# Weight tiles that are split two split tiles ahead, in a two-block transformer kernel

## What is computed

```python
mod = einsum('bd,de->be', silu(c), w_ada) + b_ada         # 48 modulation tiles, "ada"
h = modulate(rms_norm(x, norm1_w), shift1, scale1)
q, k, v, r, a_lr, su, sv, g_a, g_b = split(h @ w_in)
o_gla = rms_norm(gla_chunked(q, k, v, log_a)) * silu(r)
o_sgu = spatial_gating(gelu(su), gelu(sv), ...)
x = x + gate1 * ((sigmoid(g_a) * o_gla + sigmoid(g_b) * o_sgu) @ w_out)
x = x + gate2 * peer(modulate(rms_norm(x, norm2_w), shift2, scale2), ...)
# second block, for each of two layers l
mod   = silu(c_2) @ w_ada_2[l] + b_ada_2[l]               # 48 tiles per layer, "ada2"
mod_c = silu(c_ctx_2) @ w_ada_2[l] + b_ada_2[l]           # from the same tiles
...
x = x + gt_f * rms((silu(hf @ w_gate) * (hf @ w_up)) @ w_down, g_ffn_post)
```

## Time and profile before

| | us |
|---|---|
| median of 3 runs | 2558.24 (2558.07 to 2560.07) |
| the profiled execution | 2554.62 |
| its span, first to last instruction | 2552.9 |
| PE busy | 2240.4 |
| DVE busy | 1735.4 |
| ACT busy | 1151.7 |
| mean granted TensorE clock | 0.93 of full |

### The profile page before, as it was taken

One profiled execution on the slowest core, in us unless ns is written; L12 is line 12 of the kernel. 1 busy time (PEld: TensorE's weight loads), 2 busy tenths in 40 slices (PEclk: granted clock), 3 DMA queues, 4 the chain that ended last, 5 costly groups with the idle time before them and its releaser, 6 DMA issues.

```text
span 2552.9 us, 37972 instructions
## 1 busy us (share of the span) xinstructions
PE 2240.4 (88%) x14746; PEld 2009.0 (79%) x14746; DVE 1735.4 (68%) x3402; ACT 1151.7 (45%) x1907; POOL 53.4 (2%) x65
## 2 busy tenths in 40 slices
PE   3897789999999999988878789699979978797997
PEld 3887689999988888887757566599879967566996
DVE  5665558889988887767675565577666665664554
ACT  2532244555555554534344345444444444354443
POOL 1000000000000000000000000000000000000000
PEclk9998889999999999989977869799999999898999
DMA  7636545664468887767532100377657743102653
GB/s 278 196 127 205 177 147 180 220 218 135 145 197 283 268 278 235 245 188 227 181 126 77 35 33 17 124 229 235 213 183 246 256 160 115 58 1 89 186 187 117
DMA packets 137971, 435.04 MB, mean 170 GB/s; under 512 B 15360, under 2 KB 38144, under 8 KB 137280
## 3 DMA queue, kind: packets, MB, share of 16 engines
q1 hardware_dynamic: 109424, 396.93, 48.1%
q10 hardware_dynamic: 25776, 23.97, 2.8%
q0 software_dynamic: 2592, 11.70, 1.2%
HBM read 418.91 MB, written 13.63 MB: 169 GB/s over the span
## 4 chain that ended last, share of the span: by engine, by line
PE 65%; DVE 14%; issue 10%; ACT 7%; DMA 3%; POOL 1%; ACTq 0%; POOLq 0%; DVEq 0%; SPq 0%
PE bk L1650 63%; DVE SPL L1082 4%; PE bk L1656 3%; ACT SPL L737 2%; DVE R L1082 2%; ACT R L739 1%; DVE R L1091 1%; ACT R L737 1%; DVE ST L1097 1%; DVE RAW L1116 1%; POOL ST L639 1%; DMA RAW<-in_ada 1%; DVE R L1088 1%; DVE R L1086 1%; DMA RAW<-in_peer 1%
## 5 line engine op out<-in xcount | busy, mean ns | idle before, releaser
L1082 DVE TENSOR_TENSOR SPL<-RAW,SPL 128x1024 fp32r<-128x1024 f32 (+1 forms) x614 | 742.7, 1219 | 388.2 <-ACT SPL L737 387.2
L737 ACT ACTIVATE SPL<-RAW 128x1024 fp32r<-128x1024 f32 (+1 forms) x614 | 638.8, 1051 | 387.9 <-PE bk L1650 294.5
L1650 PE MATMUL bk<-HH,SPL 128*128 128x256 f32 x3840 | 753.3, 290 | 47.0 <-DVE SPL L1082 38.5
L1650 PEld LDWEIGHTS bk<-HH,SPL 128*128 128x128 f32 x3840 | 623.9, 195 | 61.0 <-issue 30.0
L1650 PE MATMUL bk<-SPL,WHL 128*128 128x512 f32 x2328 | 553.2, 392 | 13.2 <-DVE SPL L1082 9.5
L1650 PE MATMUL bk<-HL,SPL 128*128 128x256 f32 x1920 | 548.7, 286 | 0.0
L1650 PEld LDWEIGHTS bk<-SPL,WHL 128*128 128x128 f32 x2328 | 431.2, 189 | 103.7 <-issue 13.1
L1650 PE MATMUL bk<-SPL,HH 128*128 128x256 f32 (+1 forms) x1664 | 335.0, 303 | 62.9 <-DVE SPL L1082 48.3
L1650 PEld LDWEIGHTS bk<-HL,SPL 128*128 128x128 f32 x1920 | 374.3, 195 | 1.9 <-issue 0.2
L1650 PEld LDWEIGHTS bk<-SPL,HH 128*128 128x128 f32 x1664 | 285.2, 211 | 72.9 <-issue 55.9
L737 ACT ACTIVATE R<-bk 128x512 f32<-128x512 f32 (+5 forms) x376 | 186.6, 508 | 341.1 <-PE bk L1650 309.9
(11 more groups left out here) (126 smaller groups left out, 1993.6 us busy)
## 6 DMA issues: line engine op xcount, KB each, us to landing
RAW<-in_peer SPq DMA_DIRECT2D x256, 512.0 KB, 4.8
RAW<-in_ada SPq DMA_DIRECT2D x144, 512.0 KB, 4.7
RAW<-in_ffn SPq DMA_DIRECT2D x132, 512.0 KB, 4.0
RAW<-in_win SPq DMA_DIRECT2D x96, 512.0 KB, 4.4
RAW<-in_ffd SPq DMA_DIRECT2D x66, 512.0 KB, 4.2
RAW<-in_wout SPq DMA_DIRECT2D x32, 512.0 KB, 4.0
kept<-TMP ACTq DMA_DIRECT2D x88, 128.0 KB, 3.4
TMP<-kept ACTq DMA_DIRECT2D x66, 128.0 KB, 5.3
```

The source lines that it names most:

```text
L737: ins = e.activation(out, in_, func, bias=bias, scale=scale)
L1082: e.tensor_tensor(out, a, b, op).then_inc(*dve.up(*points))
L1650: ins = e.matmul(out, lhsT, rhs, start=start, stop=stop, skip_group_check=True)
```

## The change

The lead is counted in split tiles. `PASSED[n]` is the number of split tiles up to place n, and the new function `lead(n)` gives the place behind the second split tile after n, but not more than NRAW places on. Modulation tiles in between are prepared along the way and don't count. Ahead of the first split tile the old rule stays. Both loops, on ACT and on DVE, use it; the branch for the early PEER steps gets a `max`.

```diff
+import itertools
...
 SPLIT_NO = {n: k for k, n in enumerate(SPLITS)}
+PASSED = list(itertools.accumulate(IS_SPLIT))
+
+
+def lead(n):
+
+    return min(SPLITS[min(PASSED[n] - 1 + LEAD, len(SPLITS) - 1)], n + NRAW) + 1 if PASSED[n] else n + LEAD + 1
...
-                ahead = max([ahead] + [n + LEAD + 1 for n in CHUNKS[step]])
+                ahead = max([ahead] + [lead(n) for n in CHUNKS[step]])
...
                 if step[0] != "pe":
-                    ahead = max([ahead] + [n + LEAD + 1 for n in CHUNKS[step]])
+                    ahead = max([ahead] + [lead(n) for n in CHUNKS[step]])
                 elif step[2] == 2:
-                    ahead = CHUNKS[("pe", step[1], 0)][0] + LEAD + 1
+                    ahead = max(ahead, lead(CHUNKS[("pe", step[1], 0)][0]))
```

## The result

The changed kernel takes **2497.61 us** (median of 4 runs, 2494.03 to 2500.03) against 2558.15 us (4 runs, 2556.24 to 2560.07) on the same chip: a ratio of 0.9762, 95% interval 0.9745 to 0.9779. That is 60.5 us less. The profiled executions differ by 57.6 us (2554.62 and 2496.97). The forecast was 2505 with a range of 2486 to 2528, so direction and time came out as forecast. It will turn out that three of its terms did not.

The account below looks back on a forecast made before the run. The prediction took PE's waits for split weight tiles, in the gates caused by order, as the bound. Gains of 33 + 2.4 + 6 + 6 + 6 = 53 us from the median 2558.2 gave 2505 us, range 2486 to 2528.

Parts of the forecast that it names:

- What bounds the kernel, and the gates: Gates r1 to gb3: order bounds, not an engine; 11 periods shrink from 10.4 to 7.4 us, gaining 33 us.
- the ring: RAW slots in the gates: landing, copy, subtraction, then next load; claimed as next bound, 7.4 us per turn.
- Behind the last gate: Two wout subtractions ahead of A2 and the merges now run under gb3's matmuls: 2.4 us, 0 if late.
- v and sv: First projections: of 8.4 us of waits, only steps next to a modulation tile are cured: 6 us, 2 to 8.
- Peer alone: PEER from 735 to 975 us: PE is full already, so 32 moved tiles buy nothing.
- (d): Peer onward: moved subtractions delay hidden activations on DVE; half of 183 tiles costing PE loses 104 us: 2620; chance 0.04.
- Woven part: PEER woven with context projections, 60 moved tiles: 2 us at the longest wait plus 4 elsewhere: 6 us, -3 to 12.
- Output projection and FFN: Layer 0, 91 moved tiles: about 2 us at each of two long waits, plus small waits: 6 us, -3 to 12.
- (a): Quick transfers: landing falls to 3.6 us; gates gain 44 to 48, peer and FFN 10 each: 2485; chance 0.12.
- (b): Slow transfers: landing stays 5.8 us, a turn takes 8.6, woven stages give nothing: 26 us gained, 2532; chance 0.13.
- (c): Gates as forecast, late stages nothing at all: 41 us gained, 2517; chance 0.17.
- (e): Whole kernel: slots in use hold the tiles back, so time stays within 0.2%, 2558; chance 0.01.

Follow-up runs that it names:

- woven_only: New lead only for places 325 to 461 (PEER woven with the context's projections), old lead elsewhere, against the kernel before: 2538.81 us, ratio 0.9937.

## Why the prediction was right, and where it was not

**What bounds the kernel, and the gates.** Right, with its mechanism: the ring took over from order. The sum of a turn was 4.6 + 1.06 + 1.24 + 0.5 = 7.4. Measured were 5.1 to 5.2 + 1.07 + 1.24 + 0.1 = 7.6. Over all steps the period was 7.7, with landings of 4.7 to 6.5 us in the chain shown. Two of the sum's terms were off, against each other. The landing was taken from the v stage in the belief that spread loads land faster; but the gates moved 276 GB/s, near the 283 that the forecast itself had worked out, and the landing stayed at the 5.1 of before. The handovers cost a fifth of what was put down. The windows give 87.05 us for 11 steps that took 115.83, so 28.8 us with the tail instead of 35.4. The estimate of 3.2 us that the prediction sets beside its rows rests on a fit that the Trainium skill (DMA: Bandwidth & Descriptors, "Anatomy of one DMA") gives for DMAs that GpSimd issues. The ring's loads are issued by SP, so their 3.6 to 5.8 us don't speak against it, and the prediction should not have held it against them.

**Behind the last gate** 1.3 us instead of 2.4; **v and sv** 6.1 us, where 6 was said.

**Peer alone: the step that failed.** "PE is full already, and 32 moved tiles buy nothing there" took a full PE as a reason for zero, and it is a reason only against a gain. The loss that it left out was the forecast's own rival (d), a subtraction ahead of `ph`, in small. It had been dismissed because PE waited just 1.7 us for `WHL` before and the activation is made two tiles ahead. Neither says how much slack lies between a buffer's release and the reload that needs it. Before, DVE waited 21 times for `TMP`, 0.7 us on average: the reloads were on the edge already, and the row was there to be read. (d)'s mark was that waits for `WHL`, `HL` or `HCL` grow by over 10 us in all. They grew by 13.5 (DVE's `WHL` 10.3, ACT's 1.0, `HCL` 3.1, `HL` 0.9 less), so by its own sign (d) had begun. The price per moved tile was 12.4 / 32 = 0.39 us (0.28 by the least loss of the four traces), a third of the 1.14 that (d) assumed, and through ACT's queue, not through DVE's time.

**Woven part.** "Of the other 15 us I count 4" was the mis-sized term. The waits on `SPL` there before (992 to 1309 us); after (969 to 1268 us) they are the row of the first profile above, 13.6 us in 5, the longest 8.5:

```profile
PE bk L1650 <- DVE SPL L1082: 25.4, 27, 11.8
```

27 waits became 5. The longest shrank by 3.3, and of the 26 short ones 13.6 us came to 5.1: a gain of 8.5, not 4. On top PE's busy time is 6.1 us less (284.14, then 278.05, 1797 matmuls each). Hardly any of that is clock. The granted clock was 0.95 in both windows, and by the trace's clock records, which know two levels, full and half, the time at the half level went from 30.7 to 27.3 us, which gives back 1.7 us at most. The rest is the part of each wait that stands in the records as busy: 22 waits fewer at the 0.16 us shown above are 3.5 us (an estimate), and waits too short to show a gap can't be counted. Idle and busy time together fell by 17.2 us, the measured gain. What the forecast left out was this hidden part: it had priced only the waits that the view shows. (The expectation of `woven_only` also names the clock, which fits the gates, not this stage.)

**Output projection and FFN.** The same omission. `SPL` waits of 27.2 and 3.6 us became 11.3 and 9.9, 9.6 less in all, where 6 had been counted; PE's busy time fell by 4.5 and 1.7 us; together 15.7 of the 15.9 by which the two windows shrank. In the first part the clock can be some of it (0.94, then 0.96; 34.1 us at the half level, then 23.9), in the second it is none (0.97, then 0.96). The 7.55 stayed, as said. The wait of 4.74 us at 1796 came back as one of 3.80 us a few matmuls later.

**Rivals.** (a), (b), (c) and (e) are out by the total, (c) by the late stages too, which gave 34 us. For (d) the bound was 36 places that cost PE their time; the whole change has 183, and at 0.39 us each it would have paid back 71 us. It did so in one stage of three, the only one that reloads activations (85 loads from `kept` between 704 and 966 us, none from 970 to 1268).

**What would show it.** 7.4 us apart: 7.7. ACT's copy out of the chain: no, it stayed, with `DMA RAW` beside it, which was the sign for the ring. `SPL` waits at about 50: 55.5. Right total, then, for reasons half of which held: errors of -12.4, +11.3 and +11.2 in the late stages, -5.5 in the gates and behind them, and -1.1 in attention, which cancel by chance down to 4.

## What to carry to other kernels

Where an engine is full, more work put ahead of it cannot gain, but it can lose: for each moved instruction ask which buffer is released later, who reloads it, on which queue, and what stands in that queue behind the reload. A DMA issued from a computing engine's queue, behind a wait, is a wait of that engine. A wait view shows only part of a short wait of PE, since the record of the matmul ahead covers its start: here 27.0 us of busy time came back beside 45.1 us of waits on `SPL`. In the gates it was mostly clock, in the later stages to a good part hidden waiting.

## What the hardware showed that was not expected

A load of 512 KB from `in_win` took 5.1 us (median) from issue to landing at 205 GB/s in bursts of four, and the same 5.1 us at 276 GB/s with the loads spread out; only the modulation tiles', last in the burst, fell from 5.8 to 5.0. Spreading bought rate, hardly a shorter landing. It fell to 4.4 us when half of the other loads' bytes were gone (222 GB/s), and a load of 256 KB took 3.5 us (median). All with up to four in flight.

In the gates the granted clock went from 0.83 to 0.94 of full as the wait on `SPL` in each step (11 waits, 32.3 us) became 7 waits with 14.4 us. PE's busy time for the same 528 recorded matmuls went from 81.54 to 69.70 us: By the clock records the time at the half level fell from 39.5 to 10.3 us, which gives back up to 14.6 us. So 11.8 of the 28.8 us gained there are busy time, and most of that is clock, not waiting. The forecast had priced the step by its period and so had this inside its 33.

In the woven part the clock hardly moved, and PE's busy time fell all the same, since a matmul's record of 0.28 us reaches 0.16 us beyond the start that the next one could have. Starts over 0.3 us after the one ahead went from 54 to 30 there, and these distances fell by 20.0 us in sum.
